# Forgetting attention: two PSUM banks by turns for the value passes, two in place of three for the transposed probabilities

## Chip, cores and metric

The kernel runs on one core of a Trainium2 chip. The metric is the device time of one launch in microseconds (us), lower is better.

## What is computed

A trunk of two layers over 1024 positions of width 1024 in float32. Layer 0 mixes the positions with banded sliding-window attention, layer 1 with forgetting attention, 16 heads of width 64. Each layer then has a SwiGLU feed-forward part. The change touches only the forgetting attention:

```python
s = jnp.einsum('bqhd,bkhd->bhqk', qb, k) * scale        # qb: 128 queries of a head
s = s + cb[..., None] - cum_k[:, :, None, :]            # cumulative log forget gates
s = jnp.where(k_pos <= q_pos, s, NEG_INF)               # causal
p = jax.nn.softmax(s, axis=-1)
o = jnp.einsum('bhqk,bkhd->bqhd', p.astype(v.dtype), v)
```

## The kernel before

Float32 accuracy comes from splitting each operand into a high part that the matrix engine takes exactly and a low part, the rest. Most products are so made of two or three passes.

A head is a unit `u`; `e` is 0 for the even and 1 for the odd head of a pair, `pi` the pair. The eight query tiles of 128 rows are taken in six steps `s`: tiles (0, 1), (2, 3), 4, 5, 6, 7. Every engine runs its own queue in order, and the queues are written out by hand: the first and the last pair unrolled, the six pairs between as a loop. In the loop of step i of a pair

- TensorE (`pair_pe`) transposes the probabilities of the step, computes the raw scores four steps ahead (`qk`), and makes the value pass (`pv`) of the step before, if that one completes a group;
- ScalarE (`pair_act`) copies the transposed probabilities out of PSUM, rounded, as their high part (`probs_high`, L901), takes the exponentials three steps ahead (`exps`, L878), writes the high part of an older result (`result_high`, L913), and copies one half of the newest value pass out of PSUM (`move`, L927);
- VectorE (`pair_dve`) subtracts to get the low part of the transposed probabilities (`probs_low`, L1339), makes the biased scores and their maxima four steps ahead (`scores`, L1300), the reciprocals three steps ahead (`inverse`, L1323), the low part of an older result (`result_low`, L1351), and adds the two halves of the newest value pass (`join`, L1367);
- GpSimd (`norm_probs`, L716) multiplies the exponentials by the reciprocal.

A group is 256 queries of a head, two tiles: groups 0, 1, 2, 3 are complete after steps 0, 1, 3 and 5. Its value pass multiplies `[v high | v low]` (128 columns) with the high and the low probabilities and leaves two halves in rows 0 to 63 and 64 to 127 of a PSUM bank. `move` copies the one, `join` adds it to the other. All four groups use one bank (`O_BANK`, bank 6), so `pv` waits at its start until the group before has been joined (`fox_joined`, in `pv`).

The transposed probabilities go through PSUM in fills of at most four 128x128 blocks, each in a bank of its own. A head has 11 fills: one (3 blocks) in step 0, and two in each later step: 3+4, 4+1, 4+2, 4+3, 4+4 blocks. The 22 fills of a pair take banks 4, 5, 7 by turns (`turns`); the last of the 22 is given bank 5, so that the next pair can begin with bank 4 again. `transposes` waits before a fill until the low part of the last fill of that bank has been taken (`t_free`, raised at the end of a fill's L1339). With three banks that is as a rule the fill three back, for the last fill of a pair, the one two back.

Banks 0 to 3 hold the scores, two steps by turns.

Of the kernel before, what the change touches and what calls it, by code (L numbers as in the profile page):

```python
# [10 lines left out]
ACT = mybir.ActivationFunctionType  # L11
# [3 lines left out]
P = 128  # L15
# [21 lines left out]
def trunk(nc, x, norm_mix, norm_ffn, swa_w_in, swa_sinks, swa_w_out, fox_w_in, fox_f_bias, fox_w_out,  # L37
# [5 lines left out]
    with ctx:  # L43
# [20 lines left out]
        v_low_part = [at(f"v_low_part{i}", 56 + i, [P, 2 * P]) for i in range(2)]  # L64
        joint = [at(f"joint{i}", 58 + i, [P, 2 * P]) for i in range(2)]
# [105 lines left out]
        bank = [psum[:, i * HALF:(i + 1) * HALF] for i in range(8)]  # L171
# [103 lines left out]
        def wait(eng, s, value):  # L275

            if not (isinstance(value, int) and value <= 0):
                eng.wait_ge(s, value)
# [59 lines left out]
        class Attention:  # L338
            def __init__(self, name):
                self.fox = name == "fox"  # L340
                self.units = FOX_H if self.fox else SWA_KV
                self.qk, self.v = (fox_qk, fox_v) if self.fox else (swa_qk, swa_v)
                self.qk_dmas, self.v_dmas = (6, 2) if self.fox else (6, 4)

                self.qk_in = [sem(f"{name}_qk_in{e}") for e in range(2)]
                self.v_in = [sem(f"{name}_v_in{e}") for e in range(2)]
                self.qk_done = sem(f"{name}_qk_done")
                self.max_done = sem(f"{name}_max_done")
                self.exp_done = sem(f"{name}_exp_done")
                self.sum_done = sem(f"{name}_sum_done")  # L350
                self.inv_done = sem(f"{name}_inv_done")
                self.norm_done = sem(f"{name}_norm_done")
                self.t_done = sem(f"{name}_t_done")
                self.ph_done = sem(f"{name}_ph_done")
                self.t_free = sem(f"{name}_t_free")
                self.pv_done = sem(f"{name}_pv_done")
                self.oh_done = sem(f"{name}_oh_done")
                self.o_free = sem(f"{name}_o_free")

                self.tiles = [(0, 1), (2, 3), (4,), (5,), (6,), (7,)] if self.fox else [(t,) for t in range(TT)]  # L360
                self.steps = len(self.tiles)
                self.rings = 6 if self.fox else 4

                self.ahead = dict(qk=4, scores=4, exps=3, inverse=3, norm=3) if self.fox else \
                    dict(qk=3, scores=3, exps=2, inverse=1, norm=1)


                self.blocks = [[[(0, 0, 1), (1, 0, 2)]], [[(2, 0, 3)], [(3, 0, 4)]]] + \
                    [[[(t, 0, 4)], [(t, 4, t - 3)]] for t in range(4, TT)] if self.fox else [[1]] + [[0, 1]] * (TT - 1)
                self.fills = [len(b) for b in self.blocks]  # L370
                self.unit_fills = sum(self.fills)
                self.groups = TT // 2 if self.fox else TT

                n = 2 * self.unit_fills
                self.turns = [T_BANKS[i % 3] for i in range(n)]
                if n % 3 == 1:
                    self.turns[-1] = T_BANKS[1]

            def count(self, u, s):
# [11 lines left out]
            def bank_of(self, u, e, s, j):  # L391


                f = self.fill(u if isinstance(u, int) else e, s) + j
                n = len(self.turns)
                ago = next(d for d in range(1, n) if self.turns[(f - d) % n] == self.turns[f % n])
                return bank[self.turns[f % n]], ago

            def group(self, s):

# [6 lines left out]
        T_BANKS = (4, 5, 7)  # L407
        O_BANK = 6
# [3 lines left out]
        fox_joined = sem("fox_joined")  # L412
# [24 lines left out]
        def rows(e):  # L437
            return slice(e * HD, (e + 1) * HD)
# [380 lines left out]
        def _(act):  # L819
# [85 lines left out]

            def result_high(a, u, e, s, pi):
                g = a.group(s)
                pb = bank[O_BANK]
                if a.fox:

                    act.wait_ge(fox_joined, a.groups * u + g + 1)
                    apart(act)
                    nc.scalar.activation(o_hi[g // 2][rows(e), bass.ds(pi, 1), g % 2 * 2 * P:(g % 2 + 1) * 2 * P],  # L913
                                         joint[g % 2][rows(e), :].unsqueeze(1), ACT.Copy).then_inc(a.oh_done, 1)
                else:
                    act.wait_ge(a.pv_done, a.groups * u + g + 1)
                    for r in range(2):
                        last = nc.scalar.activation(
                            o_hi[s // 4][rows(r), 2 * u:2 * u + 2, s % 4 * P:(s % 4 + 1) * P],
                            pb.rearrange("p (a b q) -> p a b q", a=2, b=2)[rows(r), :, r, :], ACT.Copy)  # L920
                    last.then_inc(a.oh_done, 1)

            def move(a, u, e, s, pi):

                g = a.group(s)
                act.wait_ge(a.pv_done, a.groups * u + g + 1)
                nc.scalar.activation(v_low_part[g % 2][rows(0), :], bank[O_BANK][rows(1), 0:2 * P], ACT.Copy)\  # L927
                    .then_inc(fox_moved, 1)

            def pair_act(a, pi, first, last):  # L930
# [289 lines left out]
        def _(dve):  # L1220
            V = nc.vector
# [122 lines left out]

            def result_low(a, u, e, s, pi):
                g = a.group(s)
                pb = bank[O_BANK]
                dve.wait_ge(a.oh_done, a.groups * u + g + 1)
                if a.fox:
                    at0 = (rows(e), bass.ds(pi, 1), slice(g % 2 * 2 * P, (g % 2 + 1) * 2 * P))  # L1350
                    V.tensor_tensor(o_lo[g // 2][at0], joint[g % 2][rows(e), :].unsqueeze(1), o_hi[g // 2][at0].bitcast(FP32),  # L1351
                                    ALU.subtract).then_inc(a.o_free, 1)
                else:
                    for r in range(2):
                        at0 = (rows(r), slice(2 * u, 2 * u + 2), slice(s % 4 * P, (s % 4 + 1) * P))
                        last = V.tensor_tensor(o_lo[s // 4][at0],
                                               pb.rearrange("p (a b q) -> p a b q", a=2, b=2)[rows(r), :, r, :],
                                               o_hi[s // 4][at0].bitcast(FP32), ALU.subtract)
                    last.then_inc(a.o_free, 1)

            def join(a, u, e, s, pi):

                g = a.group(s)
                dve.wait_ge(fox_moved, a.groups * u + g + 1)

                wait(dve, a.o_free, a.groups * u + g - 1)
                V.tensor_tensor(joint[g % 2][rows(e), :], bank[O_BANK][rows(0), 0:2 * P], v_low_part[g % 2][rows(0), :],  # L1367
                                ALU.add).then_inc(fox_joined, 1)

            def pair_dve(a, pi, first, last):  # L1370
# [353 lines left out]
        def _(pe):  # L1724
# [150 lines left out]
            def pv(a, u, e, s, pi):  # L1875
                g = a.group(s)
                par, t = g % 2, a.tiles[s][-1]
                pb = bank[O_BANK]

                pe.wait_ge(a.t_free, a.fill(u, s) + a.fills[s])  # L1880
                wait(pe, fox_joined if a.fox else a.o_free, a.groups * u + g)
                if g == 0:

                    pe.wait_ge(a.v_in[e], 8 * a.v_dmas * (u - e + 2))
                if a.fox:
                    terms = [(k, k, slice(0 if k < t else P, 2 * P)) for k in range(t + 1)]
                    ph, pl, v = fox_p_hi[par], fox_p_lo[par], fox_operands(u, e)[3]
                    for i, (vt, pt, cs) in enumerate(terms):

                        T.matmul(pb[:, cs], v[:, vt, :], ph[:, pt, cs], start=i == 0, stop=False)  # L1890
                        last = T.matmul(pb[:, cs], v[:, vt, :], pl[:, pt, cs], start=False, stop=i == len(terms) - 1)  # L1891
                else:
                    terms = [(t - 1 + j, j, slice(0, HALF)) for j in range(0 if t else 1, 2)]
                    ph, pl, vh, vl = swa_p_hi[par], swa_p_lo[par], v_hi[e], v_lo[e]
                    for i, (vt, pt, cs) in enumerate(terms):
                        T.matmul(pb[:, cs], vh[:, vt, :], ph[:, pt, cs], start=i == 0, stop=False)
                        T.matmul(pb[:, cs], vh[:, vt, :], pl[:, pt, cs], start=False, stop=False)
                        last = T.matmul(pb[:, cs], vl[:, vt, :], ph[:, pt, cs], start=False,
                                        stop=i == len(terms) - 1)
                last.then_inc(a.pv_done, 1)  # L1900
# [221 lines left out]
```

## Time and profile before

| | us |
|---|---|
| median of 3 runs | 2486.77 |
| lowest, highest | 2485.86, 2491.13 |
| profiled execution, its own time | 2491.87 |
| its span | 2490.1 |
| TensorE busy in the span | 2339.4 (94%) |
| VectorE busy | 1398.7 (56%) |
| ScalarE busy | 987.2 (40%) |
| GpSimd busy | 589.5 (24%) |

The forgetting attention lies at about 1425 to 1690 us of the span. Engines are named PE (TensorE's multiplications), PEld (its weight loads), DVE (VectorE), ACT (ScalarE) and POOL (GpSimd). A line of the timeline merges neighbouring instructions of one kind: x2 stands for two. "Idle before <-X" is idle time of the engine that ended with X.

### The profile page before, as it was taken

The numbers are of one execution on the slowest core, as the hardware profiler recorded it, in microseconds if no ns is written. First come the engines' busy times: TensorE is split into PE (matmuls) and PEld (weight loads), VectorE is DVE, ScalarE is ACT, GpSimd is POOL, SyncE is SP. The second block draws the span as 40 slices with busy tenths as digits, with TensorE's granted clock in tenths as the row PEclk, the third lists the DMA queues.
The fourth block names the chain that finished last, engine by engine and source line by source line (L and its number), as shares of the span: only waits on it lengthen the run. The fifth ranks groups of instructions, "written<-read, shape, count | busy, mean of one in ns | idle before, by whom it ended". The sixth has DMA issues, their size and how long they took to land.

```text
span 2490.1 us, 33386 instructions
## 1 busy us (share of the span) xinstructions
PE 2339.4 (94%) x11220; PEld 1930.0 (78%) x11220; DVE 1398.7 (56%) x2204; ACT 987.2 (40%) x1884; POOL 589.5 (24%) x419
## 2 busy tenths in 40 slices
PE   4998979899999999999999989989889999999998
PEld 3776767688888878887888778877678888878887
DVE  7797954864544443433633489994584444453432
ACT  3116953443333331232212289983343333331223
POOL 3222431233322200020000056652222233200011
PEclk8999999999999999999999999999989999999999
DMA  5258543232222162222444587746313222334311
GB/s 186 89 160 207 107 135 103 68 102 76 76 89 88 59 242 92 88 97 74 144 136 152 174 189 173 173 94 194 110 51 100 77 76 80 97 127 165 114 51 76
DMA packets 306742, 291.82 MB, mean 117 GB/s; under 512 B 64992, under 2 KB 270176, under 8 KB 301680
## 3 DMA queue, kind: packets, MB, share of 16 engines
q1 hardware_dynamic: 286464, 233.99, 33.0%
q10 hardware_dynamic: 20208, 56.92, 6.2%
q8 instruction: 40, 0.66, 0.1%
q14 instruction: 30, 0.25, 0.0%
HBM read 209.02 MB, written 81.85 MB: 117 GB/s over the span
## 4 chain that ended last, share of the span: by engine, by line
PE 77%; DVE 14%; ACT 4%; issue 2%; DMA 2%; POOL 1%; ACTq 1%; SPq 0%; DVEq 0%
PE psum L1986 11%; PE psum L1988 11%; PE psum L1990 11%; PE psum L1738 10%; PE psum L1739 10%; PE psum L1740 10%; PE psum L1872 2%; DVE work_b L1629 2%; PE psum L1964 2%; PE psum L1890 2%; PE psum L1965 2%; PE psum L1966 2%; PE psum L1891 1%; PE psum L1839 1%; PE psum L1840 1%
## 5 line engine op out<-in xcount | busy, mean ns | idle before, releaser
L1986 PE MATMUL psum<-b_hi,a_hi 128*128 128x512 f32 x1232 | 484.8, 393 | 20.1 <-DVE b_lo L1457 20.1
L1988 PE MATMUL psum<-b_lo,a_hi 128*128 128x512 f32 x1232 | 482.8, 392 | 0.0
L1990 PE MATMUL psum<-b_hi,a_lo 128*128 128x512 f32 x1232 | 482.6, 392 | 0.0
L1986 PEld LDWEIGHTS psum<-b_hi,a_hi 128*128 128x128 f32 x1232 | 233.4, 189 | 71.8 <-issue 23.0
L1738 PE MATMUL psum<-set_hi,dw_hi 128*128 128x512 f32 x704 | 274.7, 390 | 3.1 <-DVE set_lo L1491 3.1
L1740 PE MATMUL psum<-set_hi,dw_lo 128*128 128x512 f32 x704 | 273.9, 389 | 0.0
L1739 PE MATMUL psum<-set_lo,dw_hi 128*128 128x512 f32 x704 | 273.9, 389 | 0.0
L1990 PEld LDWEIGHTS psum<-b_hi,a_lo 128*128 128x128 f32 x1232 | 233.4, 189 | 49.4
L1988 PEld LDWEIGHTS psum<-b_lo,a_hi 128*128 128x128 f32 x1232 | 233.6, 190 | 48.6 <-issue 0.4
L716 POOL TENSOR_TENSOR score<-score,inv_l 128x128 f32<-128x128 f32 (+7 forms) x128 | 155.2, 1223 | 379.8 <-DVE inv_l L1323 379.6
L750 POOL TENSOR_TENSOR a_sum<-a_raw 128x512 f32<-128x512 f32 x88 | 115.8, 1316 | 508.6 <-DVE a_lo L1452 440.2
L1738 PE MATMUL psum<-h_hi,w_hi 128*128 128x512 f32 x544 | 216.1, 397 | 14.5 <-DVE w_lo L1226 14.5
L1740 PE MATMUL psum<-h_hi,w_lo 128*128 128x512 f32 x544 | 213.7, 393 | 0.0
L1739 PE MATMUL psum<-h_lo,w_hi 128*128 128x512 f32 x544 | 213.7, 393 | 0.0
L1405 DVE TENSOR_TENSOR x_t<-psum,x_t 128x512 f32<-128x512 f32 x96 | 66.1, 690 | 237.1 <-PE psum L1740 226.3
L1452 DVE TENSOR_TENSOR a_lo<-a_sum,a_hi 128x512 fp32r<-128x512 f32 x176 | 129.8, 738 | 100.7 <-ACT a_hi L1016 100.5
L1016 ACT ACTIVATE a_hi<-a_sum 128x512 fp32r<-128x512 f32 x176 | 110.0, 627 | 128.6 <-PE psum L1990 126.9
L1738 PEld LDWEIGHTS psum<-set_hi,dw_hi 128*128 128x128 f32 x704 | 132.1, 188 | 33.9 <-DVE set_lo L1491 6.6
L1740 PEld LDWEIGHTS psum<-set_hi,dw_lo 128*128 128x128 f32 x704 | 132.1, 188 | 27.4
L1739 PEld LDWEIGHTS psum<-set_lo,dw_hi 128*128 128x128 f32 x704 | 132.1, 188 | 27.1
L830 ACT ACTIVATE dw_hi<-dw_raw 128x1024 fp32r<-128x1024 f32 x50 | 52.8, 1056 | 227.6 <-PE psum L1740 200.6
L824 ACT ACTIVATE w_hi<-w_raw 128x1024 fp32r<-128x1024 f32 x66 | 69.3, 1050 | 170.5 <-PE psum L1740 162.8
(207 smaller groups left out, 4437.3 us busy)
## 6 DMA issues: line engine op xcount, KB each, us to landing
a_raw<-in_ffn_w_gate_up SPq DMA_DIRECT2D x88, 512.0 KB, 5.1
hid_scr<-hid_out SPq DMA_DIRECT2D x44, 512.0 KB, 5.7
set_full<-hid_scr SPq DMA_DIRECT2D x22, 1024.0 KB, 6.5
x_t<-x_scr SPq DMA_DIRECT2D x16, 1024.0 KB, 7.2
dw_raw<-in_ffn_w_down SPq DMA_DIRECT2D x32, 512.0 KB, 4.1
x_scr<-x_t ACTq DMA_DIRECT2D x24, 512.0 KB, 2.6
w_raw<-in_fox_w_in SPq DMA_DIRECT2D x22, 512.0 KB, 4.0
w_raw<-in_swa_w_out SPq DMA_DIRECT2D x16, 512.0 KB, 4.1
```

The lines of the kernel that those rows point to most:

```text
L716: last = nc.gpsimd.tensor_tensor(sc, sc, inv_l[sl][:, i:i + 1].to_broadcast([P, fox_w(t)]), ALU.mult)
L750: nc.gpsimd.tensor_tensor(a_sum[dst][:, :, :], in0, in1, op).then_inc(a_summed, 1)
L824: nc.scalar.activation(w_hi[p][:, :, :], w_raw[p][:, :, :], ACT.Copy).then_inc(w_high, 1)
L1016: nc.scalar.activation(a_hi[i][:, :, :], a_block(q, i), ACT.Copy).then_inc(a_high, 1)
L1405: V.tensor_tensor(xs, bank[2 * p + h].unsqueeze(1), xs, ALU.add).then_inc(evac_done, 1)
L1452: V.tensor_tensor(a_lo[i][:, :, :], a_block(q, i), a_hi[i][:, :, :].bitcast(FP32), ALU.subtract)\
L1738: T.matmul(bank[2 * p + h], whi[:, k, :], mh[:, k, half(h)], start=i == 0, stop=False)
L1739: T.matmul(bank[2 * p + h], whi[:, k, :], ml[:, k, half(h)], start=False, stop=False)
L1740: last = T.matmul(bank[2 * p + h], wlo[:, k, :], mh[:, k, half(h)], start=False, stop=i == n - 1)
L1986: T.matmul(out_ps, a_hi[i][:, j, :], b_hi[i][:, j, :], start=not more and j == 0, stop=False, skip_group_check=True)
L1988: T.matmul(out_ps, a_hi[i][:, j, :], b_lo[i][:, j, :], start=False, stop=False, skip_group_check=True)
L1990: last = T.matmul(out_ps, a_lo[i][:, j, :], b_hi[i][:, j, :], start=False, stop=j == KH - 1, skip_group_check=True)
```

## The change

The forgetting attention's value passes take banks 6 and 7 by turns, group by group, and no longer wait for the join of the group before but for the one two before. Bank 7 is taken away from the transposed probabilities: their fills use banks 4 and 5 by turns, so every fill waits for the low part of the fill two back. The sliding-window attention keeps its three banks and its one.

```diff
@@ -372,8 +372,8 @@
                 n = 2 * self.unit_fills
-                self.turns = [T_BANKS[i % 3] for i in range(n)]
-                if n % 3 == 1:
+                self.turns = [T_BANKS[i % (2 if self.fox else 3)] for i in range(n)]
+                if not self.fox and n % 3 == 1:
                     self.turns[-1] = T_BANKS[1]
@@ -395,6 +395,10 @@
+            def o_bank(self, g):
+
+                return bank[O_BANK + (g % 2 if self.fox else 0)]
@@ result_high, result_low, pv @@
-                pb = bank[O_BANK]
+                pb = a.o_bank(g)
@@ move @@
-                nc.scalar.activation(v_low_part[g % 2][rows(0), :], bank[O_BANK][rows(1), 0:2 * P], ACT.Copy)\
+                nc.scalar.activation(v_low_part[g % 2][rows(0), :], a.o_bank(g)[rows(1), 0:2 * P], ACT.Copy)\
@@ join @@
-                V.tensor_tensor(joint[g % 2][rows(e), :], bank[O_BANK][rows(0), 0:2 * P], v_low_part[g % 2][rows(0), :],
+                V.tensor_tensor(joint[g % 2][rows(e), :], a.o_bank(g)[rows(0), 0:2 * P], v_low_part[g % 2][rows(0), :],
@@ pv @@
                 pe.wait_ge(a.t_free, a.fill(u, s) + a.fills[s])
-                wait(pe, fox_joined if a.fox else a.o_free, a.groups * u + g)
+                if a.fox:
+                    wait(pe, fox_joined, a.groups * u + g - 1)
+                else:
+                    wait(pe, a.o_free, a.groups * u + g)
```

## Rows read from the trace of the kernel before

**Rows 1.** Busy time by engine in 16 us of forgetting attention (start:end, length, each engine's busy us):

```profile
1546.00:1562.00 16.00, 15.17 (x115) 13.20 (x115) 15.55 (x44) 15.40 (x37) 10.24 (x9) 1.00 0.75 169
```

**Rows 2.** The waits in the forgetting attention, 1432 to 1692 us: us in total, times, longest:

```profile
ACT v_low_part L927 <- PE psum L1891: 21.1, 25, 6.6
PE psum L1890 <- DVE joint L1367: 15.9, 15, 1.5
...
PEld psum L1872 <- DVE fox_p_lo L1339: 4.1, 8, 2.5
DVE fox_p_lo L1339 <- ACT fox_p_hi L901: 3.5, 11, 0.7
```

**Rows 3.** TensorE's timeline (start us, length, what, idle before it): value passes after a join:

```profile
1564.52 0.39 PE L1890 MATMUL psum<-fox_p_hi,fox_values 128*128 128x256 f32 x1 [1.28 <-DVE joint L1367]
...
1595.05 0.39 PE L1890 MATMUL psum<-fox_p_hi,fox_values 128*128 128x256 f32 x1 [1.27 <-DVE joint L1367]
```

**Rows 4.** TensorE's weight loads for the transposes, same timeline:

```profile
1567.15 0.75 PEld L1872 LDWEIGHTS psum<-ident,score 128*128 128x128 f32 x7
...
1571.71 0.32 PEld L1872 LDWEIGHTS psum<-ident,score 128*128 128x128 f32 x3
...
1585.53 0.42 PEld L1872 LDWEIGHTS psum<-ident,score 128*128 128x128 f32 x4 [0.25 <-DVE fox_p_lo L1339]
1586.73 0.31 PEld L1872 LDWEIGHTS psum<-ident,score 128*128 128x128 f32 x3
```

**Rows 5.** VectorE, groups by shape, 1456 to 1657 us: the 512-wide low-part subtraction (count, total, mean ns):

```profile
L1339 DVE TENSOR_TENSOR fox_p_lo<-psum,fox_p_hi 128x512 fp32r<-128x512 f32 x79 | 53.1, 686 | 2.8 <-ACT fox_p_hi L901 1.6
```

**Rows 6.** VectorE's timeline, even head's end and odd head's end:

```profile
1565.73 0.15 DVE L1323 RECIPROCAL inv_l<-psum_l 128x1 f32<-128x1 f32 x1
1565.81 0.40 DVE L1351 TENSOR_TENSOR o_lo<-joint,o_hi 64x256 f32 x1
1566.80 1.02 DVE L1339 TENSOR_TENSOR fox_p_lo<-psum,fox_p_hi 128x512 fp32r<-128x512 f32 x2 [0.26 <-ACT fox_p_hi L901]
1571.44 1.29 DVE L1339 TENSOR_TENSOR fox_p_lo<-psum,fox_p_hi 128x512 fp32r<-128x512 f32 x2
...
1575.53 0.40 DVE L1367 TENSOR_TENSOR joint<-psum,v_low_part 64x256 f32<-64x256 f32 x1
1576.02 1.18 DVE L1339 TENSOR_TENSOR fox_p_lo<-psum,fox_p_hi 128x384 fp32r<-128x384 f32 x2
...
1584.32 1.16 DVE L1339 TENSOR_TENSOR fox_p_lo<-psum,fox_p_hi 128x512 fp32r<-128x512 f32 x2
1586.82 1.29 DVE L1339 TENSOR_TENSOR fox_p_lo<-psum,fox_p_hi 128x512 fp32r<-128x512 f32 x2
...
1591.28 0.42 DVE L1367 TENSOR_TENSOR joint<-psum,v_low_part 64x256 f32<-64x256 f32 x1
1591.73 1.16 DVE L1339 TENSOR_TENSOR fox_p_lo<-psum,fox_p_hi 128x384 fp32r<-128x384 f32 x2
```

**Rows 7.** ScalarE's timeline in the same stretch:

```profile
1565.06 0.40 ACT L913 ACTIVATE o_hi<-joint 64x256 f32 x1
...
1575.09 0.38 ACT L927 ACTIVATE v_low_part<-psum 64x256 f32<-64x256 f32 x1 [0.42 <-PE psum L1891]
1575.50 0.98 ACT L901 ACTIVATE fox_p_hi<-psum 128x384 fp32r<-128x384 f32 x2
...
1590.40 0.38 ACT L927 ACTIVATE v_low_part<-psum 64x256 f32<-64x256 f32 x1 [0.24 <-PE psum L1891]
```

**Rows 8.** GpSimd's timeline: the multiplication that follows the reciprocal at 1565.73:

```profile
1565.96 2.00 POOL L716 TENSOR_TENSOR score<-score,inv_l 128x1024 f32<-128x1024 f32 x1 [0.41 <-DVE inv_l L1323]
```

**Rows 9.** VectorE, the one long low-part subtraction of a result:

```profile
1672.28 1.98 DVE L1351 TENSOR_TENSOR o_lo<-joint,o_hi 64x256 fp32r<-64x256 f32 x1 [0.28 <-ACT o_hi L913]
```

**Rows 10.** GpSimd, what it ran at that time:

```profile
1670.18 3.79 POOL L716 TENSOR_TENSOR score<-score,inv_l 128x896 f32<-128x896 f32 x2 [1.30 <-DVE inv_l L1323]
```

**Rows 11.** TensorE's weight loads, the transposes of the last head:

```profile
1675.48 0.31 PEld L1872 LDWEIGHTS psum<-ident,score 128*128 128x128 f32 x3 [2.46 <-DVE fox_p_lo L1339]
```

More of the change, by code:

```diff
@@ L1346, in result_low @@
                 g = a.group(s)
-                pb = bank[O_BANK]
+                pb = a.o_bank(g)
                 dve.wait_ge(a.oh_done, a.groups * u + g + 1)
@@ L1877, in pv @@
                 par, t = g % 2, a.tiles[s][-1]
-                pb = bank[O_BANK]
+                pb = a.o_bank(g)
                 pe.wait_ge(a.t_free, a.fill(u, s) + a.fills[s])
-                wait(pe, fox_joined if a.fox else a.o_free, a.groups * u + g)
+                if a.fox:
+                    wait(pe, fox_joined, a.groups * u + g - 1)
+                else:
+                    wait(pe, a.o_free, a.groups * u + g)
                 if g == 0:
```

## The prediction

> **What bounds the kernel now.** The page shows TensorE busy for 94% of the span, which says little about this change: it touches one stage of some 265 us. So the first view is the busy time of that stage alone. In 16 us of it VectorE is busy for 15.55, ScalarE for 15.40, TensorE for 15.17 [rows 1]. The reader is to see that VectorE is full: 0.45 us in 16 are all that it can give back, over the stage of 265 us some 7 us. TensorE is the least full of the three.
>
> The second view is the list of waits in the stage. TensorE stands 15.9 us in 15 waits for the join of L1367 before a value pass [rows 2], mostly once per head: group 1 is ready one step after group 0, and the bank is not free. The timeline shows such waits of 1.28 and 1.27 us, 30.53 us apart, which is one pair of heads [rows 3]. That is the wait which the change removes. The same list shows what it adds: TensorE already waits now and then for the low part of a fill (4.1 us in 8 waits) [rows 2], and VectorE waits for the high parts 3.5 us in 11 times [rows 2].
>
> The third view is the timeline of each engine over one pair, from the group 1 pass of one even head to that of the next. I name the heads by where VectorE's work lies in it: the last steps of an even head, then those of an odd one.
>
> **The part that is removed.** The value pass of group 1 can start about 1.3 us earlier in each head. Who needs it earlier? ScalarE's copy of L927 stands behind it, then the high parts of the next step, then VectorE. In the even head VectorE waits there for 0.26 us (at 1566.80) [rows 6] and again 0.09 us ahead of 1576.02 (the join at 1575.53 ends at 1575.93) [rows 6]. In the odd head it shows no such wait. So the removal can give VectorE at most 0.35 us per pair, 8 pairs: 2.8 us. The rest of TensorE's 15.9 us is idle time of an engine that isn't the last one, and buys nothing.
>
> **The part that is added: a fill waits for the fill two back.** The kernel before has this wait in one place, the last fill of a pair. There the low parts of the fill two back end at 1584.32 + 1.16 = 1585.48 [rows 6], and the weight load of the fill follows at 1585.53, after 0.25 us idle [rows 4]. So the price is known: the transposes start 0.05 us behind the subtraction that they wait for, and nothing of that wait is hidden on TensorE.
>
> I went through the 11 fills of a head, comparing the start of each with the end of the subtraction two fills back. Most are late enough. The one that matters is the only fill of step 0, three blocks. It comes directly after the two fills of step 5, and now waits for the first of those. Its place is bad, for TensorE's longest piece lies behind it: the scores, the value pass of group 3 with 16 multiplications, and only then L927, the high parts and VectorE.
>
> - End of an even head. The first subtraction of step 5 starts at 1571.44 [rows 6] and a 512-wide one takes 0.69 us [rows 5]. So the fill can be loaded at 1571.44 + 0.69 + 0.05 = 1572.18; it is loaded at 1571.71 now [rows 4]. It moves by 0.47. Behind it TensorE has no idle time until the copy at 1575.09, for which ScalarE waits [rows 7]; the high parts start at 1575.50 [rows 7] and VectorE's subtraction at 1576.02, for which VectorE waits [rows 6]. All of that moves by 0.47 us, with nothing to hide it.
> - Does 1571.44 itself come earlier, since VectorE saves its 0.26? It can start step 3's subtraction at 1566.80 - 0.26 = 1566.54, which ends at 1567.23; the transposes of step 4 now wait for this, until 1567.28. They are loaded at 1567.15 today [rows 4]. So they don't get earlier, and what comes behind them (the value pass of group 2, its copy, the high parts of step 5) doesn't either. The gain of 0.26 is lost again inside the head, and I take 1571.44 as it stands.
> - End of an odd head. The fill can be loaded at 1586.82 + 0.69 + 0.05 = 1587.56 in place of 1586.73 [rows 4, 6], 0.83 later. But here the way from the load to the copy is 1590.40 - 1586.73 = 3.67 us, against 1575.09 - 1571.71 = 3.38 in the even head [rows 4, 7]: 0.29 us of it is waiting of the value pass for its own low parts, and hides as much. The copy moves by 0.54 to 1590.94, and VectorE's subtraction, 1576.02 - 1575.09 = 0.93 behind it, to 1591.87. It starts at 1591.73 now without waiting (the join at 1591.28 ends at 1591.70) [rows 6]: 0.14 us.
> - The other late fills (first of step 4 in the odd head, by about 0.8 us) move TensorE's queue too, with the scores behind them. The scores are made four steps ahead, and the copy of group 2 finds ScalarE still busy; VectorE doesn't see it. I cost them at nothing; if that cover is gone they cost up to what the step 0 fill costs in the odd head.
> - The last head. The transposes of step 4 wait there 2.46 us for a subtraction before their last three blocks [rows 11]. With two banks the first four blocks wait for the same one. Four weight loads take 0.42 us [rows 4], and TensorE ends this stage, so 0.42 is paid in full.
>
> There are 15 changes of head: 8 from an even to an odd one and 7 back. **Sum:** 8 x 0.47 + 7 x 0.14 + 0.42 = 3.8 + 1.0 + 0.4 = 5.2 us. No instruction is added or taken away, and no queue gets a step moved; the DMA loads of the heads hang on the same counts and are issued well ahead. Against the profiled execution that is 2491.87 + 5.2 = 2497.1; this one run is 5.1 us over the median of the three, and the change in the median is the same sum: 2486.8 + 5.2 = 2492.0. From below the sum is bounded by the even head's 0.47 being half hidden, 2.5 us in all, from above by the odd head costing 0.47 too, 7.5 us.
>
> **Rivals.** (1) *The new waits are hidden* by the slack that TensorE gains from the join, and VectorE keeps its 0.35 us per pair. For it: TensorE has 1.3 us more per head. Against: the fill waits for VectorE, not for TensorE's own work, so being earlier doesn't help it. The time is 2486.8 - 2.8 = 2484.0 to 2487.
>
> (2) *The result's low part falls behind GpSimd.* VectorE's L1351 for group 0 starts at 1565.81 behind the reciprocal of 1565.73, and GpSimd starts at 1565.96 a multiplication of 2.00 us that hangs on the same reciprocal [rows 6, 8]. Normally VectorE is first. Once in the trace it is not: at 1672.28 it had to wait 0.28 us for ScalarE, found GpSimd at work from 1670.18 to 1673.97, and took 1.98 us, until GpSimd was done, where 0.40 is usual [rows 6, 9, 10]. The page "SBUF — State Buffer" of the Trainium skill ("Who interferes with whom") says why: a VectorE instruction with two inputs in SBUF and a GpSimd one that reads SBUF exclude each other, and whoever starts first holds on to the end. By that rule the trace agrees. Now the margin: ScalarE's L913 ends at 1565.46 [rows 7], one pair later at 1595.99, and hangs on the copy of 1590.40, which moves by 0.54: 1596.53. VectorE wants to start L1351 at 1565.81 + 30.53 + 0.14 = 1596.48 and can at 1596.53 + 0.05 = 1596.58; GpSimd starts at 1596.48 + 0.15 = 1596.63. That is 0.05 us to spare, less than I can read off. If it is lost, each of 7 pairs pays about 1.95 us more: 13.7 us, and the time is 2505.6. The point from which it decides is a delay of 0.6 us of the copy in place of 0.54.
>
> (3) *TensorE's wait for the join does set the end*, as the chain of waits suggests, which runs through it. Then its 15.9 us go and nothing comes: 2470.9. Against it: VectorE has only 0.45 us free in 16 [rows 1]. The realistic part of it is the 7 us that VectorE has.
>
> **How the numbers follow.** Forecast 0.60, 2492.0, own range 2489.3 to 2494.3; rival 1 0.15; rival 2 0.18; rival 3 0.07. A run of this kernel can tell 0.2%, 5.0 us, from no change, so the border lies at 2491.8, almost on the forecast. I give slower 0.32 of the forecast's 0.60 and all of rival 2: 0.50. Same: 0.28 of the forecast and rival 1: 0.43. Faster: rival 3, 0.07. The range takes in rivals 1 and 2: 2484 to 2506.
>
> **What would show it.** Right: no wait of L1890 for L1367 any more; in its place waits of the transposes (L1872) for L1339, some 0.5 to 1 us at each change of head; VectorE's wait for L901 grows by about 0.4 us per pair; the distance of two pairs' group 1 passes grows from 30.53 to about 31.1 us. Rival 2 shows as L1351 with durations near 2 us in the middle of the stage. Wrong would be a pair of 30.2 us or less, or VectorE with more than 1 us idle per pair.

## The result, and the profile after

The changed kernel takes 2515.1 us (median of four runs, 2512.38 to 2518.25) against 2487.55 before: a ratio of 1.0109, 95% interval 1.0092 to 1.0127, so 27.5 us slower by the medians. The forecast was 2492.0 with a range up to 2506: the sign was right, the time lies above the range, and the loss is over five times the 5.2 us of the sum. Rival 2, given 0.18, is what happened, and more than rival 2.

The profiled execution (its own time 2512.38) has a span of 2510.6 us, 20.5 us over that of before. Outside the forgetting attention little moved: its first transposes start 2.4 us earlier (1425.84 in place of 1428.29), and what comes behind it is 0.6 us shorter. First the list of waits in the stage, 1432 to 1720 us (us in total, times, longest). The lines of the code have moved: L1876 are the transposes, L1343 the low parts of the probabilities, L1371 the join, L931 ScalarE's copy.

```profile
PE psum L1876 <- DVE fox_p_lo L1343: 34.6, 46, 3.0
ACT v_low_part L931 <- PE psum L1898: 31.4, 24, 6.3
PEld psum L1876 <- DVE fox_p_lo L1343: 31.2, 36, 2.3
DVE joint L1371 <- ACT v_low_part L931: 15.9, 21, 3.7
```

The reader is to compare with [rows 2]: TensorE's 15.9 us for the join are gone, not one is left. In their place it waits 34.6 us for the low parts of the fill two back. ScalarE's wait for the value pass grew from 21.1 to 31.4 us, and VectorE now stands 15.9 us ahead of its join, in 21 waits, where the list of before (1432 to 1692 us) has 7.9 in three:

```profile
DVE joint L1367 <- ACT v_low_part L927: 7.9, 3, 3.7
```

The group of result low parts, 1432 to 1710 us (count, total, mean ns, idle time before):

```profile
L1355 DVE TENSOR_TENSOR o_lo<-joint,o_hi 64x256 f32 x48 | 30.0, 625 | 1.5
```

At 0.41 us each they took 19.7 before. The 10 us more are six instructions, one in each pair of the loop. (A seventh long one, of 1.98 us, lies in the last head, as it did before [rows 9].) Here is one of them with what stood around it, in the timelines of VectorE, ScalarE and GpSimd:

```profile
1572.62 0.15 DVE L1327 RECIPROCAL inv_l<-psum_l 128x1 f32<-128x1 f32 x1
...
1572.33 0.40 ACT L917 ACTIVATE o_hi<-joint 64x256 f32 x1
...
1572.85 1.89 POOL L720 TENSOR_TENSOR score<-score,inv_l 128x1024 f32<-128x1024 f32 x1 [0.41 <-DVE inv_l L1327]
...
1572.90 2.12 DVE L1355 TENSOR_TENSOR o_lo<-joint,o_hi 64x256 f32 x1
```

This is the picture that the prediction drew from [rows 6 to 8], with the order of the last two turned round: GpSimd starts 0.05 us before VectorE, and VectorE's 0.4 us become 2.12. ScalarE's part was done at 1572.73, only about 0.03 after VectorE could have used it. It starts 0.16 later for another reason, which the same line's sequencer rows tell (count, ns min/median/max, first and last start), first of after around 1572.9, then of before around 1565.8:

```profile
L1355 DVEq FUSED_REGOPS  x1: 79/79/79, 1572.8 to 1572.8; - x1
```

```profile
L1351 DVEq FUSED_REGOPS  x1: 79/79/79, 1565.5 to 1565.5; - x1
```

In the loop the address of that instruction is worked out in registers, 0.08 us, after the wait for ScalarE. Before, the wait was over early and this was done at 1565.5, while the engine was still at other work. Now it lies on the path. In all six cases this register work lies between ScalarE's end and VectorE's start, and these are 0.15 to 0.16 us apart; VectorE starts 0.04 to 0.05 us behind GpSimd.

Last, the transposes. The weight loads of the step 0 fill mark the changes of head; every other one is a pair:

```profile
1514.79 0.31 PEld L1876 LDWEIGHTS psum<-ident,score 128*128 128x128 f32 x3 [0.34 <-DVE fox_p_lo L1343]
...
1547.88 0.31 PEld L1876 LDWEIGHTS psum<-ident,score 128*128 128x128 f32 x3 [0.34 <-DVE fox_p_lo L1343]
...
1582.56 0.31 PEld L1876 LDWEIGHTS psum<-ident,score 128*128 128x128 f32 x3 [0.34 <-DVE fox_p_lo L1343]
```

A pair takes 33.09 or 34.68 us where it was 30.53 [rows 3]. The six pairs with a long subtraction come in these two lengths, three of each (the first of the short ones takes 33.26). What tells them apart is the stretch behind the transposes of step 4, for which TensorE waits 2.26 us in all six, since the long subtraction stands ahead of the one they need:

```profile
1475.16 0.75 PEld L1876 LDWEIGHTS psum<-ident,score 128*128 128x128 f32 x7 [2.26 <-DVE fox_p_lo L1343]
...
1508.25 1.36 PEld L1876 LDWEIGHTS psum<-ident,score 128*128 128x128 f32 x7 [2.26 <-DVE fox_p_lo L1343]
```

The windows of 4 us there (start:end, length, busy us of PE, PEld, DVE, ACT, POOL, then the granted clock):

```profile
1475.00:1479.00 4.00, 3.84 (x33) 3.76 (x33) 4.00 (x14) 2.98 (x9) 1.20 (x3) 1.00 1.00 246
1508.00:1512.00 4.00, 3.75 (x18) 3.56 (x19) 3.70 (x11) 2.57 (x7) 1.08 (x2) 0.57 1.01 242
1542.70:1546.70 4.00, 3.80 (x33) 3.72 (x33) 4.00 (x14) 2.99 (x9) 1.16 (x3) 1.00 0.98 247
1575.80:1579.80 4.00, 3.79 (x18) 3.60 (x19) 3.94 (x13) 2.53 (x7) 1.08 (x2) 0.58 1.02 243
1610.50:1614.50 4.00, 3.82 (x18) 3.63 (x19) 3.71 (x11) 2.50 (x7) 1.08 (x2) 0.57 1.01 247
1645.00:1649.00 4.00, 3.68 (x31) 3.60 (x32) 4.00 (x14) 2.98 (x9) 1.08 (x2) 1.00 1.00 250
```

In three of the six the granted clock is 0.57 or 0.58 in that window, which mixes the full 2.4 GHz with the lower level of 1.2; there TensorE gets through 18 multiplications instead of 31 to 33. Those are the three pairs of 34.65 to 34.68 us. Before, the clock was 1.00 through this part of the stage.

### The profile page after: what moved, and what is told of

Its sections match the earlier page's. It is cut to its first block, busy times and chain, and to the rows that moved or that the text cites. A ratio compares the mean times of both kernels' runs of the same rounds, so it can differ in the third digit from the quotient of the medians.

```text
span 2510.6 us, 33355 instructions
## 1 busy us (share of the span) xinstructions
PE 2342.0 (93%) x11220; PEld 1932.5 (77%) x11220; DVE 1410.0 (56%) x2204; ACT 988.8 (39%) x1884; POOL 590.2 (24%) x419
## 4 chain that ended last, share of the span: by engine, by line
PE 75%; DVE 15%; ACT 4%; issue 3%; DMA 1%; POOL 1%; ACTq 1%; SPq 0%; DVEq 0%; POOLq 0%
PE psum L1993 11%; PE psum L1997 11%; PE psum L1995 11%; PE psum L1742 10%; PE psum L1744 10%; PE psum L1743 10%; PE psum L1876 2%; DVE work_b L1633 2%; PE psum L1971 1%; PE psum L1972 1%; PE psum L1973 1%; PE psum L1897 1%; PE psum L1898 1%; DVE w_lo L1230 1%; DVE fox_p_lo L1343 1%
## 5 line engine op out<-in xcount | busy, mean ns | idle before, releaser
L1876 PE MATMUL psum<-ident,score 128*128 128x128 f32 x816 | 118.9, 285 | 45.5 <-DVE fox_p_lo L1343 34.6
```

Source lines behind the costliest of these rows:

```text
L1876: last = T.transpose(tb[:, b * P:(b + 1) * P], score[sl][:, at0:at0 + P], ident[:, :])
```

## The experiments

My theory after the result: the late step 0 fill moves ScalarE against VectorE, VectorE then loses the race against GpSimd once per pair, and the rest follows. The rivals: the waits for two banks are the loss by themselves; or it is the second bank of the value passes, which lets TensorE run ahead. Pairs are measured as above, between the weight loads of the step 0 fill.

### One part alone: two banks for the transposes

```diff
-                self.turns = [T_BANKS[i % 3] for i in range(n)]
-                if n % 3 == 1:
+                self.turns = [T_BANKS[i % (2 if self.fox else 3)] for i in range(n)]
+                if not self.fox and n % 3 == 1:
```

> One part of the change alone: the transposed probabilities take banks 4 and 5 by turns, the value passes keep their one bank and their old wait for the join. Theory (the fewer banks of the transposes cost, the second bank of the value passes buys nothing): within 5 us of the changed kernel, 2510 to 2520 us, with six low-part subtractions of a result near 2 us in the loop. Rival (the second bank lets TensorE run ahead and that is what upsets the order): 2490 to 2495 us, no long subtraction in the loop.

Measured: 2508.1 us, ratio 1.0078 (1.0059 to 1.0096), six long subtractions in the loop; the time is 2 us under the theory's range. Two of them, from VectorE's timeline, and the windows behind the transposes of step 4 in the fifth and the sixth:

```profile
1539.08 2.13 DVE L1351 TENSOR_TENSOR o_lo<-joint,o_hi 64x256 f32 x1
...
1572.19 2.12 DVE L1351 TENSOR_TENSOR o_lo<-joint,o_hi 64x256 f32 x1
```

```profile
1608.20:1612.20 4.00, 3.81 (x33) 3.73 (x33) 4.00 (x14) 2.98 (x9) 1.17 (x3) 1.00 1.01 250
1641.30:1645.30 4.00, 3.81 (x20) 3.62 (x20) 3.83 (x13) 2.40 (x7) 1.17 (x3) 0.61 1.02 250
```

A pair takes 33.10 us, as the shorter ones of after, and one in six is longer. So the fewer banks alone bring most of the loss. The second bank of the value passes does not come out at nothing, as I wrote, it costs: the whole change is about 7 us slower than this part. With it TensorE no longer stops at the join, reaches the transposes of step 4 earlier and stands there in one piece, 2.26 us, where here it stands 1.89 us and the rest ahead of the join; the clock falls in three of six pairs there, in one of six here. These are two profiles, one of each kernel; that the longer stand makes the clock fall more often is my reading, and no run takes the clock away by itself.

### Taking the race away in the changed kernel: ScalarE's order

```diff
+                    if a.fox and (done := a_done(a, pi, i - 1, first)):
+                        result_high(a, *done)
                     if ahead := a_step(a, pi, i + a.ahead["exps"], last):
                         exps(a, *ahead)
-                    if done := a_done(a, pi, i - 1 if a.fox else i, first):
+                    if not a.fox and (done := a_done(a, pi, i, first)):
                         result_high(a, *done)
```

> The changed kernel, with ScalarE writing the high part of an older result ahead of the exponentials in place of behind them, so that it is done over 1 us before VectorE wants it. Theory (VectorE's subtraction loses a race of some 0.1 us against GpSimd, and this with what it sets off is over half of the loss): no subtraction of about 2 us in the loop; 2492 to 2499 us. Rival (the waits for two banks are the loss, the long subtractions fall into time that VectorE would wait anyway): 2508 us or more.

Measured: 2505.0 us, 1.0066 (1.0049 to 1.0083). No subtraction over 0.50 us is left, 10 us came back, but the time misses the theory's range from above. So the exchange needed a control, in the kernel before.

> Control of after_hi_first: the same exchange on ScalarE (high part of the older result ahead of the exponentials) in the kernel before, which has no long subtraction in its loop. It tells what the exchange itself costs, since it puts the exponentials 0.4 us later and VectorE's reciprocal waits for them. Theory (after_hi_first lost its time to the exchange): 8 to 12 us slower than before, so that the changed banks without the lost race cost some 5 to 8 us. Rival (the exchange is free and the two-bank waits cost 16 us by themselves): within 3 us of before.

Measured: 2493.1 us, 1.0019 (1.0009 to 1.0029), between the two expectations. The control's profile names the price:

```profile
DVE inv_l L1325 <- ACT score L878: 6.5, 15, 0.9
```

VectorE's reciprocal waits for the exponentials. A pair takes 31.42 us with the exchange and the old banks, 32.43 with the new: the banks without the race cost 1.01 us per pair and 11.9 us in the medians, above the 5 to 8 that I had expected.

### The same on VectorE

```diff
+                    if a.fox and (done := a_done(a, pi, i - 1, first)):
+                        result_low(a, *done)
                     if a.fox and (ahead := a_step(a, pi, i + a.ahead["inverse"], last)):
                         inverse(a, *ahead)
-                    if done := a_done(a, pi, i - 1 if a.fox else i, first):
+                    if not a.fox and (done := a_done(a, pi, i, first)):
                         result_low(a, *done)
```

> VectorE makes the low part of the older result ahead of the reciprocal in place of behind it, in the kernel before: the reciprocal releases GpSimd only then, so the race can't be lost. Control for the next run. Theory: within 3 us of before, since before has no lost race in its loop. Rival (VectorE then waits for ScalarE's high part at each group): 5 us or more slower.

> The same exchange on VectorE in the changed kernel. Theory (the two-bank waits cost about 5 us, the lost race and what follows it the rest): no subtraction of 2 us, a pair of heads takes 31.0 to 31.4 us, and the time lies 5 to 9 us over before_low_first. Rival (the race matters little): 15 us or more over it.

Measured: the control 2486.2 us, 0.9990 (0.9980 to 0.9999); the changed kernel with it 2499.2 us, 1.0038 (1.0026 to 1.0051). The long subtractions are gone, and this second way of taking the race away brings 16 us back. But 13.0 us over the control is above the 5 to 9 expected: 31.74 us a pair against 30.61. VectorE's timeline over one such pair shows four waits:

```profile
1538.35 0.42 DVE L1355 TENSOR_TENSOR o_lo<-joint,o_hi 64x256 f32 x1 [0.21 <-ACT o_hi L917]
...
1544.24 1.29 DVE L1343 TENSOR_TENSOR fox_p_lo<-psum,fox_p_hi 128x512 fp32r<-128x512 f32 x2 [0.26 <-ACT fox_p_hi L905]
...
1548.77 0.42 DVE L1371 TENSOR_TENSOR joint<-psum,v_low_part 64x256 f32<-64x256 f32 x1 [0.37 <-ACT v_low_part L931]
...
1564.82 0.42 DVE L1371 TENSOR_TENSOR joint<-psum,v_low_part 64x256 f32<-64x256 f32 x1 [0.21 <-ACT v_low_part L931]
```

The two at the join are the changes of head, 0.37 and 0.21 where the prediction had 0.47 and 0.14. The wait of 0.21 for ScalarE's high part of a result is not in its sum. The one of 0.26 for the high parts of the probabilities is no new wait: it stands in the kernel before [rows 6] and in the control, and is the one that the second bank of the value passes should have taken away.

```profile
1537.69 1.02 DVE L1339 TENSOR_TENSOR fox_p_lo<-psum,fox_p_hi 128x512 fp32r<-128x512 f32 x2 [0.22 <-ACT fox_p_hi L901]
```

The pairs are not all of the 13 us. Between the two profiled spans lie 12.4 us: 8.3 in the seven pairs and 3.9 in the last head, which takes 36.4 us (granted clock 0.87) in place of 32.6 (0.97). It is measured from its step 0 fill to the first multiplication behind the attention.

### The price of the race alone

```diff
+                    if a.fox and (done := a_done(a, pi, i, first)):
+                        join(a, *done)
                     if done := a_done(a, pi, i - 1 if a.fox else i, first):
                         result_low(a, *done)
-                    if a.fox and (done := a_done(a, pi, i, first)):
-                        join(a, *done)
```

> The kernel before with its banks, but VectorE makes the join ahead of the low part of the older result, so that a 0.4 us instruction lies between the reciprocal and that subtraction and GpSimd is always first. Nothing waits longer for banks. Theory (GpSimd's multiplication shuts the subtraction out until it ends, and VectorE has no slack for it): nearly all of the 64 subtractions take 1 to 2 us where the mean is 0.43, and the time grows by 40 to 70 us. Rival (the lock costs little on its own, the loss needs the two banks): under 10 us more.

Measured: 2526.9 us, 1.0151 (1.0128 to 1.0174), 38 us slower with the banks of before. The result low parts of its stage, the loop's and the unrolled ones:

```profile
L1351 DVE TENSOR_TENSOR o_lo<-joint,o_hi 64x256 f32 x48 | 52.0, 1084 | 0.9
L1351 DVE TENSOR_TENSOR o_lo<-joint,o_hi 64x256 fp32r<-64x256 f32 x16 | 14.7, 920 | 0.8 <-ACT o_hi L913 0.5
```

Over the usual 0.41 that is 48 x 0.67 + 16 x 0.51 = 40 us, near the 38 lost. I had expected almost all 64 to be long; the join and the low part meet in only some steps, so 30 are (1.5 to 2.0 us), and the loss lies just under my range. Not all of the 38 is the lock: the pairs between the step 0 fills show that the clock falls here too (start:end, length, busy us, then the granted clock):

```profile
1574.45:1611.50 37.05, 30.79 (x219) 26.60 (x217) 35.31 (x85) 29.59 (x74) 18.88 (x17) 0.95 0.63 142
1611.50:1646.97 35.47, 29.19 (x219) 25.04 (x217) 34.93 (x85) 29.48 (x74) 18.89 (x17) 1.00 0.66 148
```

Four of the six pairs of the loop are of the first kind (36.80 to 37.05 us), two keep the full clock (34.96 and 35.47). In the pair at 1611.50 four long subtractions take 5.4 us more than usual, and the pair is 4.9 us longer than before. So of what GpSimd takes there, VectorE pays some nine tenths, and the lower clock comes on top.

### Which fill it is

First the step 0 fill is given a bank that the value passes leave free at its time, the rest of the change stays.

```diff
-                self.turns = [T_BANKS[i % (2 if self.fox else 3)] for i in range(n)]
+                self.turns = [6, 4, 5, 4, 5, 4, 5, 4, 5, 4, 5] * 2 if self.fox else [T_BANKS[i % 3] for i in range(n)]
...
                     wait(pe, a.t_free, f - ago + 1)
+                    if a.fox and (s, j) in {(0, 0): -1}:
+                        wait(pe, fox_joined, a.groups * u + {(0, 0): -1}[(s, j)])
```

> The changed kernel, but the single fill of step 0 goes through bank 6, which the value passes leave free at that time (it waits for the join of group 2), the other ten fills take banks 4 and 5 by turns. Theory (the late fill of step 0, with the value pass of group 3 behind it, is what moves ScalarE against VectorE): no long subtraction in the loop, 2486 to 2491 us. Rival (the fills of steps 3 and 4 do it, which wait 0.5 us in the changed kernel): 2500 us or more.

Measured: 2493.0 us, 1.0014 (1.0004 to 1.0024): 3.5 us over before by the ratio and 4.5 by the medians, no long subtraction in the loop, a pair at 30.65 us. The time is 2 us above the theory's range, the mechanism as it says. TensorE still waits 19.2 us in 30 waits for low parts here, in the loop at the fills of steps 3 and 4, and against the kernel before it costs 0.1 us per pair. VectorE's wait of 0.26 for the high parts is still there too, so these fills also eat what the second bank of the value passes could give; the planned banks below show how much.

Then the opposite, one wait added to the kernel before and nothing else, without and with the harmless order on VectorE:

```diff
                     wait(pe, a.t_free, f - ago + 1)
+                    if a.fox and s == 0:
+                        wait(pe, a.t_free, f - 1)
```

> The kernel before with its three banks for the transposes and its one for the value passes, and one wait more: the single fill of step 0 also waits for the low part of the fill two back. Theory (this one wait is all that the smaller number of banks costs, and it alone makes VectorE lose the race): six subtractions of 2 us in the loop, 2506 to 2511 us as with two banks. Rival (the waits of the fills of steps 3 and 4 have their share): no lost race, or under 2500 us.

> The same added wait in before_low_first, where the race can't be lost. It gives the price of the wait alone. By the prediction's own arithmetic it is 0.61 us per pair, 5 us in all; after_low_first was 13 us over its control. Theory (the step 0 fill is the whole, and the arithmetic was short): 9 to 13 us over before_low_first, a pair at 31.6 to 31.8 us. Rival (the arithmetic was right for this fill, the other fills cost the rest): 3 to 6 us over it, a pair at 31.1 to 31.3 us.

Measured: 2502.2 us, 1.0058 (1.0040 to 1.0076), with six long subtractions and 32.72 us a pair; and 2493.7 us, 1.0014 (1.0004 to 1.0025), without any and with 31.38 us a pair. TensorE's weight loads of the second:

```profile
1542.73 0.31 PEld L1876 LDWEIGHTS psum<-ident,score 128*128 128x128 f32 x3 [0.43 <-DVE fox_p_lo L1339]
...
1558.68 0.31 PEld L1876 LDWEIGHTS psum<-ident,score 128*128 128x128 f32 x3 [0.70 <-DVE fox_p_lo L1339]
1574.10 0.31 PEld L1876 LDWEIGHTS psum<-ident,score 128*128 128x128 f32 x3 [0.42 <-DVE fox_p_lo L1339]
```

This one wait loses the race by itself, which settles the first half of the question. Its own price is 31.38 - 30.61 = 0.77 us per pair, and 7.5 us in the medians, between what the theory and its rival expected. VectorE's waits in such a pair are three of the four above, 0.37, 0.21 and 0.21; the one of 0.26 is not there. The other fills, which cost 0.1 against before once the step 0 fill is on time, add 31.74 - 31.38 = 0.36 when it is late, and with them the wait of 0.26 is back; and s0_wait stayed below the 2506 of its theory because they are missing (32.72 against 33.10, and the clock falls in none of its six pairs).

### Versions with neither price

Both value banks and no late fill: the fills also use banks 6 and 7 while these stand empty.

```diff
+                self.turns = [6, 4, 5, 4, 5, 6, 4, 7, 5, 4, 7] * 2 if self.fox else [T_BANKS[i % 3] for i in range(n)]
...
+                    if a.fox and (s, j) in {(0, 0): -1, (3, 0): 1, (4, 0): 2}:
+                        wait(pe, fox_joined, a.groups * u + {(0, 0): -1, (3, 0): 1, (4, 0): 2}[(s, j)])
```

> Both changes without their price: value passes by turns on banks 6 and 7, and the eleven fills of a head on banks 6,4,5,4,5,6,4,7,5,4,7, that is also on 6 and 7 where these stand empty (with a wait for the join that empties them). TensorE waits neither for the last join nor for a fill two back where that is late. Theory (VectorE is the last engine, TensorE's waits were idle time that nobody needed): 2483 to 2488 us, so a gain of 0 to 5. Rival (the join's wait did set the end): 2470 to 2478.

Measured: 2486.5 us, 0.9988 (0.9978 to 0.9998), a pair at 30.10 us. So this is what the change was worth had its price been avoided: 0.43 us per pair, a little above the 0.35 that I read as the most VectorE could give back. Five pairs of before and five of this run (start:end, length, busy us of PE, PEld, DVE, ACT, POOL, then the granted clock):

```profile
1480.10:1632.77 152.67, 142.18 (x1083) 125.42 (x1081) 148.33 (x421) 144.09 (x361) 97.63 (x81) 1.00 0.76 172
1479.11:1629.61 150.50, 146.44 (x1083) 126.78 (x1081) 147.94 (x421) 144.02 (x361) 97.62 (x81) 1.00 0.78 174
```

VectorE's idle time falls from 0.87 to 0.51 us per pair, by 0.36, and the rest is 0.08 us less busy time. Against after_s0_six (30.65) it is 0.55 us per pair: that is what the waits of the fills of steps 3 and 4 take, most of it the gain of the second bank and not a loss against before.

> The planned banks together with the low part ahead of the reciprocal, the two versions that came out a little under the kernel before. Theory (both only take small waits off VectorE, which is full): 2483 to 2487 us, no more than 2 us under either. Rival (the gains add up and more): under 2482 us.

Measured: 2485.0 us, 0.9985 (0.9974 to 0.9995), 30.22 us a pair. It doesn't add up to more than the planned banks alone. It is the fastest version by its ratio, 0.15% under before, which is less than the 0.2% that a run of this kernel can tell.

### VectorE relieved

The 64 subtractions of L1351 move to GpSimd, behind its multiplication, with a wait for its own last instruction on either side:

```diff
+            def pool_low(a, u, e, s, pi, normed):
+                g = a.group(s)
+                pool.wait_ge(a.norm_done, normed)
+                pool.wait_ge(a.oh_done, a.groups * u + g + 1)
...
+                nc.gpsimd.tensor_tensor(o_lo[g // 2][at0], joint[g % 2][rows(e), :].unsqueeze(1),
+                                        o_hi[g // 2][at0].bitcast(FP32), ALU.subtract).then_inc(a.o_free, 1)
```

> The kernel before with the low part of the results (64 subtractions, 27.8 us of VectorE in all) made on GpSimd, behind its multiplication. Theory (VectorE sets the end of this stage, with ScalarE close behind it at 15.40 of 16 us): 3 to 9 us faster, 2479 to 2485 us, and TensorE's wait for the join shrinks. Rival (VectorE is not the bound, TensorE's chain through the join is): within 2 us of before.

> The same move to GpSimd in the changed kernel. There is no VectorE instruction left that GpSimd can shut out. Theory: the loss shrinks from 27 us to under 8 us against before. Rival (the waits for two banks are the main loss): it stays over 12 us slower than before.

> The move to GpSimd together with the planned banks. Theory: with 27.8 us less on VectorE, TensorE's wait for the join is worth something: 2 to 6 us faster than before_pool_low. Rival (ScalarE becomes the bound at once): the same as before_pool_low within 2 us.

Measured: 2486.0 us, 0.9987 (0.9977 to 0.9997); 2499.0 us, 1.0038 (1.0024 to 1.0052); and 2487.3 us, 0.9988 (0.9978 to 0.9998). The second is the third way of taking the race away and lands 13.0 us over its control, as the one on VectorE did; my "under 8 us" was wrong for the same reason. The first lies 1 us above the theory's range, and bears the claim that VectorE sets the end only weakly: with 27.8 us off it the kernel gains about 3. The join now waits in two places:

```profile
DVE joint L1382 <- ACT v_low_part L942: 11.3, 19, 4.2
DVE joint L1382 <- POOL o_lo L730: 11.0, 14, 0.9
```

VectorE got free time and spends it waiting for ScalarE and for GpSimd's subtraction. The planned banks add nothing to that in the medians, as the rival had it. The window of five pairs of plan_pool_low:

```profile
1475.60:1626.10 150.50, 142.81 (x1083) 126.37 (x1082) 135.88 (x380) 143.98 (x361) 120.26 (x121) 1.00 0.77 174
```

With the planned banks five pairs take 150.50 us whether VectorE is busy for 147.94 of them or for 135.88. So VectorE alone does not set their length. ScalarE is busy for 144.0 in both. Whether its order is the next bound, or the new wait for GpSimd ate the gain, these runs leave open.

## Why the prediction was right or wrong

**What bounds the stage: right as far as it was used.** TensorE's waits for the join were worth little: the planned banks, which take them away without the price, give 0.43 us per pair against the 0.35 read as the most. Rival 3 falls by this, and by the result, where all 15.9 us of waiting went and the time rose. That the gain of 0.26 is lost again behind the transposes of step 4 was right too: VectorE's wait stays 0.26 in after_s0_six and is gone with the planned banks.

**The step 0 fill: right place, right order of size.** In the sum it was 0.47 + 0.14 = 0.61 us per pair. Put alone into the kernel, with the race out of the way, it cost 0.77 per pair, and giving it a free bank took nearly all of the loss away. (The lower bound of the sum was added up wrongly: with the even head's 0.47 halved it is 3.3 us, not 2.5. Nothing hangs on it.)

**The other fills: wrong.** "I cost them at nothing" holds only while ScalarE is on time. In after_s0_six they cost 0.1 us per pair against before; behind a late step 0 fill they cost 0.36. The fallback price that I gave them there, that of the odd head's step 0 fill, 0.14, was too small too. In all, the waits cost 31.74 - 30.61 = 1.13 us per pair where the sum had 0.61. I had checked each wait against the timeline of before, in which nothing is shifted, and not against the shifted one.

**The last head: too small.** It was 0.42 in the sum. From its step 0 fill to the first multiplication behind the attention it was 1663.40 to 1698.27, 34.9 us, and is 1682.18 to 1719.40, 37.2: 2.3 us longer in this one profile. The granted clock of this stretch fell from 0.94 to 0.87. With two banks for the transposes alone (t_two) it takes 35.6 us at 0.93, which is 0.7 longer, so most of the 2.3 seems to go with the lower clock; no run separates the two.

**The race (rival 2): the failed step.** The mechanism, the instruction and the count were as written, 6 of the 7 pairs that I had named. The chance was not. I found 0.05 us to spare and took 0.05 us from ScalarE's end to VectorE's start. In the loop it is 0.16, because the address is worked out behind the wait; the one case that I had as a model, at 1672.28 [rows 9], lies in the unrolled last pair, where nothing is worked out and it is 0.03. This one term decides. The rest of the working came out: it had ScalarE's end 0.13 us behind the start of the reciprocal (1596.53 against 1565.73 + 30.53 + 0.14 = 1596.40), and in the case above it is 0.11 (1572.73 against 1572.62). With 0.16 in place of 0.05 VectorE starts at 1596.69, 0.06 us behind GpSimd's 1596.63, and the race is lost by the prediction's own figures; measured, it was lost by 0.04 to 0.05. A margin smaller than the error of the terms it is made of was an even chance at best, and I gave 0.18.

**Its price: too high for the instruction, short for what hangs on it.** I added 1.95 us per loss and no more. The instruction takes 2.12 - 0.40 = 1.72 us more, and the pair pays 33.09 - 31.74 = 1.35 us net, six times, 8.1 us; s0_wait with and without the race gives the same, 32.72 - 31.38 = 1.34. Part of the 1.72 fills waits that are there anyway. But the transposes of step 4, which with two banks hang on the subtraction behind the long one, then stand 2.26 us, and in three pairs TensorE's clock falls: 34.66 - 33.09 = 1.57 us each, 4.7 us. The prediction had no line for the clock.

Together, for the seven pairs from the second head's step 0 fill to the last head's: waits 1.13 x 7 = 7.9, the race 8.1, the clock 4.7, in all 20.7. Measured they went from 213.85 us (1449.55 to 1663.40) to 235.30 (1446.88 to 1682.18), 21.4 more; 0.7 stays without a name. The last head adds 2.3. That the span grew by only 20.5 is luck of these two executions: the seven pairs begin 2.7 us earlier, and what follows the attention is 0.6 us shorter. The medians differ by 27.5, and that is the same loss: the profiled execution of before is 4.3 us above its median, and that of after 2.7 us below its own (20.5 + 4.3 + 2.7 = 27.5). How many pairs lose the clock in the executions that were not profiled isn't known.

## What to carry to other kernels

A wait that is cheap by itself can turn the order of two engines that share something: look for the places where two instructions hang on the same release and the slower must not be first, and treat a margin of a tenth of a microsecond there as a coin, the more so where a loop computes addresses behind the wait. Better, order the queues so that the race can't be lost; here that cost nothing. Before giving up a buffer for a wait that looks long, ask whether the waiting engine is the last one, and which single fill needs the buffer: it could be had from banks that stood empty for part of each head.

## What the runs showed of the hardware

- A VectorE subtraction with both inputs in SBUF that started 0.05 us behind a GpSimd multiplication of 1.89 us took 2.12 us in place of 0.40, and ended 0.28 us after GpSimd. When it started first, by 0.15 us [rows 6, 8], it took 0.40 and the multiplication 2.00. The page "SBUF — State Buffer" of the Trainium skill ("Who interferes with whom") states that a VectorE instruction with two inputs in SBUF contends with a GpSimd one that reads SBUF, for an exclusive lock, and that the order of issue decides who blocks. The traces agree.
- In the loop 0.15 to 0.16 us lie between ScalarE's end and the start of VectorE's instruction that waits for it, 0.07 to 0.08 of them register work for an address; in the unrolled pair, without that work, 0.03. When the wait was over early (1565.5 in before), the register work was hidden.
- After the same idle time of 2.26 us TensorE's granted clock stayed at 1.00 in three pairs and was 0.57 or 0.58 of full speed over 4 us in three, which made such a pair 1.57 us longer. With 1.89 us ahead of it, it fell in one of six. What the runs don't show is what decides between the two.
